# A convolution-and-attention mixer layer laid out anew: order of projections, of convolution taps and of the output rows

## The reference

```python
h = rms_norm_2(x, mix_norm[l]); proj = h @ w_in[l]
a, g, q, k, v, fl = jnp.split(proj, splits, axis=-1)      # 512 each, fl 8
# conv_module(a, g): u = a * sigmoid(g); causal depthwise convolution of 31 taps, 512 channels
#   y = layer_norm(conv(u) + conv_b); y_conv = silu(y)
# forgetting_attention(q, k, v, fl + forget_b): 8 heads of 64,
#   s = q.k/8 + cum[q] - cum[k], cum = cumsum(log_sigmoid(.)); causal softmax; p @ v
y = concat([rms_norm_2(y_conv, onc), rms_norm_2(y_attn, ona)])
x = x + y @ w_out[l]
```

## Time and profile before

| | us |
|---|---|
| median of three runs (lowest, highest) | 1084.83 (1083.31, 1086.01) |
| the profiled execution, its own time | 1083.39 |
| its span, first to last instruction | 1081.6 |
| busy in the span: TensorE, VectorE, ScalarE, GpSimd | 1036.5, 723.3, 617.5, 360.6 |

### The profile page before, as it was taken

How to read it: one execution, slowest core, us unless ns; L and a number is a source line. 1 busy time by engine, 2 the same in 40 slices (tenths; PEclk the granted TensorE clock), 3 DMA queues, 4 the chain that set the end, 5 groups by cost and what they waited for, 6 DMA issues and landing times.

```text
span 1081.6 us, 18110 instructions
## 1 busy us (share of the span) xinstructions
PE 1036.5 (96%) x7606; PEld 972.5 (90%) x7606; DVE 723.3 (67%) x961; ACT 617.5 (57%) x859; POOL 360.6 (33%) x208
## 2 busy tenths in 40 slices
PE   6999999999999899999999999999996899999997
PEld 5889999999987799999999888899986698888886
DVE  5876997773548689877547766643877678665542
ACT  6766666553446566665436555442867966555531
POOL 1062265530100025455102555400387303545400
PEclk9999999999999999999999999999998999999999
DMA  8534664546332346555453755555333155555351
GB/s 317 210 135 159 234 231 158 197 143 233 129 118 78 112 143 237 192 177 198 175 192 118 248 184 193 192 195 175 118 118 116 41 195 188 202 195 195 123 189 39
DMA packets 27297, 183.61 MB, mean 170 GB/s; under 512 B 3152, under 2 KB 3280, under 8 KB 5968
## 3 DMA queue, kind: packets, MB, share of 16 engines
q1 hardware_dynamic: 26784, 181.74, 47.5%
q10 hardware_dynamic: 432, 0.71, 0.2%
HBM read 181.39 MB, written 1.05 MB: 169 GB/s over the span
## 4 chain that ended last, share of the span: by engine, by line
PE 83%; ACT 5%; POOL 4%; DVE 4%; issue 2%; DMA 1%; SPq 0%; DVEq 0%; POOLq 0%; ACTq 0%
PE psum L289 83%; POOL Y L1882 3%; ACT Pb L1004 1%; ACT whi L898 1%; DVE Pb L1460 1%; DMA raw<-in_wst 1%; DVE wlo L1357 1%; ACT Ob L1202 1%; ACT Pb L1211 0%; DVE bias L1363 0%; DVE Pb L1360 0%; ACT L895 0%; POOL LR L1960 0%; PE psum L494 0%; ACT PT L898 0%
## 5 line engine op out<-in xcount | busy, mean ns | idle before, releaser
L289 PE MATMUL psum<-G,whi 128*128 128x256 f32 (+1 forms) x2720 | 614.7, 314 | 12.5 <-DVE wlo L1357 12.5
L1357 DVE TENSOR_TENSOR wlo<-raw,whi 128x2048 fp32r<-128x2048 f32 (+1 forms) x172 | 390.8, 2285 | 217.8 <-ACT whi L898 217.6
L289 PEld LDWEIGHTS psum<-G,whi 128*128 128x128 f32 x2720 | 447.2, 190 | 46.8 <-DVE G L1363 8.5
L289 PE MATMUL psum<-G,wlo 128*128 128x256 f32 x1712 | 482.2, 282 | 0.0
L898 ACT ACTIVATE whi<-raw 128x2048 fp32r<-128x2048 f32 (+1 forms) x172 | 318.5, 1864 | 175.2 <-PE psum L289 168.9
L289 PEld LDWEIGHTS psum<-G,wlo 128*128 128x128 f32 x1712 | 325.0, 190 | 0.1
L1882 POOL TENSOR_TENSOR Alo<-Ab,Ahi 128x512 fp32r<-128x512 f32 x44 | 124.8, 2836 | 139.6 <-ACT Ahi L898 139.6
L1882 POOL TENSOR_TENSOR Ab<-Cb 128x512 f32<-128x512 f32 x44 | 117.5, 2671 | 118.2 <-ACT Cb L939 118.2
L289 PE MATMUL psum<-Ahi,wlo 128*128 128x256 f32 x528 | 149.6, 283 | 0.0
L289 PE MATMUL psum<-Alo,whi 128*128 128x256 f32 x528 | 149.6, 283 | 0.0
L289 PE MATMUL psum<-Ahi,whi 128*128 128x256 f32 x528 | 149.6, 283 | 0.0
(11 more groups left out here) (179 smaller groups left out, 1099.5 us busy)
## 6 DMA issues: line engine op xcount, KB each, us to landing
raw<-in_wst SPq DMA_DIRECT2D x165, 1024.0 KB, 4.9
bias<-in_bias_c SPq DMA_DIRECT2D x1, 2048.0 KB, 8.0
raw<-in_wst SPq DMA_DIRECT2D x3, 512.0 KB, 7.5
X<-in_x SPq DMA_DIRECT2D x4, 256.0 KB, 6.9
raw<-in_wst SPq DMA_DIRECT2D x4, 256.0 KB, 7.1
out<-bias SPq DMA_DIRECT2D x4, 256.0 KB, 2.0
bias<-in_bias_a SPq DMA_DIRECT2D x1, 512.0 KB, 11.1
bias<-in_invcnt SPq DMA_DIRECT2D x1, 512.0 KB, 12.0
```

What stands on the lines that cost most here:

```text
L289: return pe.matmul(o, a, b, start=start, stop=stop, skip_group_check=True)
L1357: return dve.tensor_tensor(o, a, b, op)
```

## The change

Projections now go a1, a2, a0, a3, fl, q0, q1, q2, v0, q3, v1. Tiles 1 and 2 of the convolution take turns on VectorE after a lead of four taps, and VectorE makes the first 20 taps of tile 3 (`early`, in SBUF tile Y), GpSimd the last 11. The forget gate is cut into three pieces placed among the taps; GpSimd starts tile 0 before the factors. In the tail the sums are issued one tile at a time, the attention sums come first, the first rows (two attention tiles) stand between variance sums and square sums, the second behind the square sums, and the attention tiles' scaling and splitting is interleaved with the convolution's norm steps. Two more weight chunks are split ahead of the tail. The core of the diff:

```diff
-    project("w_in", (128, 640))
+    project("w_in", (128, 640), (256, 768), (0, 512), (384, 896))
     plan.append(("heads", "w_in", 2560))
-    project("w_in", (0, 512), (1024, 1536), (256, 768), (384, 896))
-    project("w_in", (1152, 1664), (1280, 1792), (1408, 1920), (2048, 2176), (2304, 2432))
+    project("w_in", (1024, 1536), (1152, 1664), (1280, 1792), (2048, 2176), (1408, 1920), (2304, 2432))
...
+LEAD = 4
+EARLY = 20
-POOL_TAPS = place(*[(0, j) for j in range(31)], *[(3, j) for j in range(30)])
-DVE_TAPS = place(*[(1, j) for j in range(31)], *[(2, j) for j in range(31)], (3, 30))
+POOL_TAPS = place(*[(0, j) for j in range(31)], *[(3, j) for j in range(EARLY, 31)])
+DVE_TAPS = place(*[(1, j) for j in range(LEAD)], *[t for j in range(31 - LEAD) for t in ((2, j), (1, j + LEAD))],
+                 *[(2, j) for j in range(31 - LEAD, 31)])
...
-                value(0)
-                score(3)
-                pe.wait_ge(s_qk, 8 + 4)
-                tokens_first(5, c0 + 10)
-                value(1)
-                turn(2)
-                pe.wait_ge(s_vt, 5)
-                sum_tiles(5, [Y[:, i, :] for i in range(4)], conv_ready, s_xs)
-                value(2)
-                turn(3)
-                sum_tiles(4, [UP[:, i, 0:S] for i in range(4)], lambda n: pe.wait_ge(s_xq, n + 1), s_xs)
-                value(3)
-                pe.wait_ge(s_ptb2, 4)
-                sum_tiles(7, [T[:, i, 0:S] for i in range(4)], lambda n: pe.wait_ge(s_o2, n + 1), s_n)
-                sum_tiles(5, [UP[:, i, 0:S] for i in range(4)], lambda n: pe.wait_ge(s_xq2, n + 1), s_xs)
+                tokens_first(4, c0 + 10)
+                score(3)
+                turn(1)
+                turn(2)
+                value(0)
+                conv_sum(0, 0)
+                value(1)
+                value(2)
+                turn(3)
+                att_sum(0)
+                att_sum(1)
+                value(3)
+                att_sum(2)
+                att_sum(3)
+                conv_sum(1, 1)
+                conv_sum(2, 2)
+                conv_sum(3, 3)
+                var_sum(0)
...
                 rows(0, 2)
+                square_sum(0)
...
                 rows(1, 3)
                 rows(2, 0)
                 rows(3, 1)
...
+                def early(j):
+                    if j == 0:
...
+                        dve.wait_ge(s_tape, j)
+                        STT(Y[:, 3, :], UP[:, 3, j:j + S], col("conv_w", 4 * j + 3), Y[:, 3, :], ALU.mult, ALU.add).then_inc(s_tape, 1)
...
+                early(13)
+                tap(1, 23)
+                early(14)
+                tap(2, 20)
...
+                att_scale(0)
+                center(0)
...
+                att_scale(1)
+                att_low(0)
+                att_scale(2)
+                spread(0)
+                att_low(1)
...
+                        if i == 3 and j == EARLY:
+                            pool.wait_ge(s_tape, EARLY)
...
+                taps(0, 0, 13)
                 pool.wait_ge(s_cum, 1)
                 factors(0)
+                taps(0, 13, 14)
                 factors(1)
+                taps(0, 14, 16)
                 factors(2)
-                taps(0, 0, 26)
+                taps(0, 16, 19)
                 factors(3)
-                taps(0, 26, 31)
-                taps(3, 0, 30)
+                taps(0, 19, 31)
+                taps(3, 20, 31)
...
+                att_factor()
+                att_high(0)
+                conv_square(0)
...
+                att_high(1)
                 conv_factor(0, 4)
+                att_high(2)
+                conv_silu(0)
...
+                att_high(3)
+                high(c0 + 14)
                 table()
                 conv_factor(1, 5)
```

More of the change, by code:

```diff
@@ L508, in values @@
                 last.then_inc(s_pv, 1)
[L510 to L514, removed]
             def l0():
@@ L1278, in mix @@
[L1278 to L1286 removed]
+                products(0, 20, 23)
+                exps(u0 + 1, 1)
+                high(c0 + 11)
+                probs(0)
+                products(0, 23, 25)
+                exps(u0 + 2, 2)
@@ new lines, in mix @@
+                high(c0 + 12)
+                turned(0)
+                products(0, 25, 28)
+                probs(1)
+                products(0, 28, 30)
+                probs(2)
+                products(0, 30, 31)
+                products(3, 20, 21)
+                turned(1)
+                act.wait_ge(s_used, USED[MIX_CHUNK["v1"]])
+                take_v(4, 1, 4)
+                exps(u0 + 3, 0)
+                products(3, 21, 23)
+                turned(2)
+                out(0)
+                high(c0 + 13)
@@ L1308, in mix @@
-                conv_factor(1, 5)
-                high(c0 + 13)
-                for i in range(4):
-                    act.wait_ge(s_on2, 4 + i + 1)
-                    copy(Mhi[:, i, :], Y[:, i, :]).then_inc(s_mh2, 1)
-                high(c0 + 14)
+                products(3, 28, 30)
+                out(3)
+                products(3, 30, 31)
+                att_factor()
+                att_high(0)
+                conv_square(0)
+                conv_square(1)
+                conv_square(2)
@@ L1772, in mix @@
-                taps(1, 21, 22)
+                tap(1, 1)
+                low(c0 + 5)
+                glu(2)
+                tap(1, 2)
+                gates(0)
+                tap(1, 3)
+                tap(2, 0)
+                tap(1, 4)
+                tap(2, 1)
+                low(c0 + 6)
+                glu(0)
+                tap(1, 5)
+                tap(2, 2)
+                tap(1, 6)
+                tap(2, 3)
+                gates(3)
+                tap(1, 7)
+                tap(2, 4)
@@ new lines, in mix @@
+                tap(1, 8)
+                tap(2, 5)
+                tap(1, 9)
+                tap(2, 6)
+                tap(1, 10)
+                tap(2, 7)
+                low(c0 + 7)
+                tap(1, 11)
+                glu(3)
+                forget_sum()
+                tap(2, 8)
+                tap(1, 12)
+                take_q(0)
+                tap(2, 9)
+                early(0)
+                tap(1, 13)
+                tap(2, 10)
+                early(1)
+                tap(1, 14)
@@ L1773, in mix @@
+                early(2)
+                forget_scan()
+                early(3)
+                columns(2)
+                early(4)
+                low(c0 + 8)
+                forget_parts()
+                early(5)
+                tap(2, 11)
+                take_q(1)
+                early(6)
+                tap(1, 15)
+                tap(2, 12)
+                early(7)
+                tap(1, 16)
+                early(8)
+                tap(2, 13)
                 bias_in(0)
-                take_q(1)
@@ L1775, in mix @@
-                glu(3)
-                low(c0 + 8)
+                take_q(2)
                 low(c0 + 9)
-                taps(1, 22, 23)
-                take_q(2)
-                columns(2)
-                taps(1, 23, 24)
+                tap(1, 17)
+                tap(2, 14)
+                tap(1, 18)
                 bias_in(1)
-                taps(1, 24, 25)
-                glu(2)
-                taps(1, 25, 26)
+                tap(2, 15)
+                tap(1, 19)
+                low(c0 + 10)
@@ L1823, in mix @@
-                for i in range(4):
-                    dve.wait_ge(s_mh2, 4 + i + 1)
-                    TT(Mlo[:, i, :], Y[:, i, :], f(Mhi[:, i, :]), ALU.subtract).then_inc(s_m2, 1)
+                tap(1, 20)
+                tap(2, 17)
+                bias_in(2)
+                low(c0 + 11)
+                take_q(3)
+                early(9)
+                tap(1, 21)
+                inverse(1)
+                early(10)
+                low(c0 + 12)
+                inverse(2)
+                tap(2, 18)
```

398 lines of the change are left out of this document (232 added, 166 removed).

## The result

The changed kernel takes 1072.26 us (median of 4 runs, 1071.79 to 1072.71) against 1084.17 (1083.31 to 1086.01) on the same chip: ratio 0.989 [0.987, 0.991], 11.9 us faster. I had said 1076, that is 7.6 us off the profiled execution of before; that profile is now 11.6 shorter. Direction and place were right; the gain is half as large again.

What follows compares the result with a forecast made beforehand. TensorE was held back by GpSimd's convolution adds and VectorE's last tap of tile 3, then by a tail of sums and norms. Middle +0.8 and tail -8.4 gave -7.6 us from 1083.39: 1076 us stated, range 1068 to 1085.

Steps and rivals of the forecast that it cites:

- Ceiling: In the changed stage of 129.4 us, 22.3 us is all that a reordering can win.
- GpSimd: Middle: 18 adds fewer, 15.8 us; start at 785.5, 7 us idle before the factors, tile 3 done at 852.0.
- VectorE: Middle: taps by turns at 0.39 instead of 0.525 us, so 19 extra taps cost nothing.
- Count to the last early tap: Middle, VectorE: its queue counted from 785.5 adds 52.3 us, giving 837.8 before contention.
- The surcharge of 2.6 for contention: Middle, VectorE: 15 early taps meet GpSimd adds at 0.17 us each, putting the last early tap at 840.4.
- The middle: From the stage's start to the end of the conv sums: almost nothing won, 854.0 against 853.2, +0.8 us.
- added 4 for the clock: Middle, TensorE's attention chain: lower clock after gaps moves the last attention sum from 848.6 to 852.6.
- The tail: After the conv sums: 29.1 us instead of 37.5, attention rows running during SiLU work, -8.4 us.
- The 1.3 for the clock at the rows' start: Tail, TensorE: 14 matmuls at the lower clock lose 0.09 us each as the rows begin.
- The first: Whole stage: TensorE bound again, few adds met, clock stays up; -12.9 us, 1070.5, down to 1068; chance 0.20.
- the second rival: Middle: ScalarE's queue as the bound, five tile-3 groups costing 1 us each, 1081 in total; chance 0.12.
- VectorE as the bound: Middle: taps stay at 0.525, early taps wait for whole adds, last early tap 857.2; +7.8 us, 1091; chance 0.09.

Runs made afterwards that it cites:

- experiment 9: The changed kernel run once more, nothing altered: 1072.53 us, ratio 0.988.
- experiment 6: The changed kernel with seven extra matmuls of constants in TensorE's two gaps of the middle: 1069.91 us, ratio 0.986.
- experiment 1: The changed kernel with VectorE's taps of tile 1 all before those of tile 2 instead of by turns: 1074.71 us, ratio 0.991.
- experiment 3: The changed kernel with TensorE's first attention rows behind the square sums instead of before them: 1078.73 us, ratio 0.995.
- experiment 5: The kernel before with only part of the tail's new order, attention rows and their inputs ahead of SiLU and squares: 1082.33 us against 1085.17, ratio 0.998.
- experiment 4: The changed kernel with 24 early taps on VectorE instead of 20 and 7 GpSimd adds of tile 3 instead of 11: 1072.85 us, ratio 0.990.
- 8: The changed kernel with 10 early taps on VectorE instead of 20 and 21 GpSimd adds of tile 3: 1078.27 us, ratio 0.994.
- 10: The changed kernel with both the seven matmuls of constants and 24 early taps, ScalarE's tile 3 products moved up: 1070.68 us, ratio 0.986.
- experiment 11: The changed kernel with constants' matmuls, 24 early taps, products moved up, and a convolution sum ahead of each of the last two attention sums: 1070.44 us, ratio 0.986.

## Why the prediction was right, and where its sizes were off

By its own steps, in its order; times of after less 1.2.

*Ceiling.* 22.3 us were to be had; 12.8 came in the profile, 11.1 in experiment 9's, 13.3 in experiment 6's.

*GpSimd.* 18 adds fewer, and 6.85 idle before the first factor, where I had 7. (The steps that I listed to its start add up to 785.05, not 785.5; it started at 785.6.) Its last add ends at 849.5, not 852.0: the last early tap came 3.2 earlier than I said, and tile 3 took 12.2, not 11.6.

*VectorE.* The pitch of 0.39 came as forecast and experiment 1 shows it (0.525 without the turn). The Trainium skill, "VectorE: DVE Perf Modes", section "The DRAIN you can't avoid", says that the next operation does not start until the pipe is empty and that a semaphore between chained copies costs nothing extra. As I had read it, the turn would win nothing; it won 2.5 us. The same section adds that a next operation that is not held starts earlier, and the gain from the turn agrees with that addition; for taps, a wait for the tap just before costs 0.13. My 8.1 for a turn that fails put 0.525 on all 60 taps; without the turn only 20 of them had it.

*Count to the last early tap.* 837.8 by the count, 837.2 measured, which is partly luck. The six low parts were counted at their mean length of 2.41 and cost 2.2 from start to start (813.38 to 815.58), 1.2 less in all, and that hides what contention did cost. The surcharge of 2.6 for contention was too large: ten early taps meet an add, not 15, and lose 0.9 together from start to next start, 0.5 of it in the one of 0.97; the first, a tensor_scalar, took 0.91 beside an add and lost 0.4 more. So 1.3. The upper bound, a whole add of 0.75 each (which the rule of "SBUF — State Buffer" in the Trainium skill, section "Who interferes with whom", gives), fits the tap of 0.97 and is far off for the other nine, with 0.47 to 0.57. That the early taps write to SBUF and the others to PSUM is not the cause: the nine early ones beside no add take 478 ns, as the others do with 480.

*The middle.* Last attention sum at 849.05; the queues' count gave 848.6, and I had added 4 for the clock. The gaps came (1.52, 2.27, 1.29 for my 1.7, 2.4, 2.3) and so did the lower clock, but only in part of the stretch, and what it cost at the end was 0.5 us in this execution and about 2 in experiment 9, measured from my count (849.31 + 1.52 less the start of 761.40 gives 89.4 after the start, against 87.75 here and 87.3 by the count); from experiment 6, with the clock at 1.00 and 86.6, it is 1.1 and 2.8. Middle: -2.8 (-1.1 in experiment 9) instead of +0.8. **This surcharge is the term that was mis-sized most**: I took the pitch of a stretch behind a gap of 7.86 for one behind gaps of about 2. It is not enough by itself: with the 4 gone, my own GpSimd, done at 852.0, would have held the centring at 852.6. The surcharge on the early taps had to be too large too.

*The tail.* -10.0 instead of -8.4. The 1.3 for the clock at the rows' start did not come: with the pause ahead of the variance sums at 1.02 the window from 851.68 has a clock of 1.00. The rest of the count was right: 27.5 for my 27.7. (The steps that make the convolution tiles ready add up to 5.3, not 5.9, so the 0.1 for them had no ground.) The one place where I saw the risk, square sums behind the first rows, is the one that experiment 3 shows to carry 6.2. What I had not seen is how much of it rests on the middle: in the old middle the same rows ahead of the square sums give 0.5 in the tail of the profile and 2.8 in the medians (experiment 5).

*The rivals.* The first had -12.9 for the stage, my own sum without its surcharges; -12.8 came in this profile and -11.1 in experiment 9's, and the median of 1072.26 lies between its 1070.5 and my 1076. The mechanism is between the two: TensorE is the bound from 852.60 on, not in the 20 us before. ScalarE's queue did not cost the 5 us that the second rival gave it: GpSimd waits 2.8 for it in all, 1.2 of that in tile 3. But the chain of waits runs through it from 821.8 to 842.4, so it is what the middle hangs on there; and at 24 early taps GpSimd waits 3.8 for it if its products are not moved up (experiment 4). VectorE as the bound did not come: its last early tap would have had to end after 849.4, and ended at 837.2.

Not settled: what the gated inputs ahead of the forget gate are worth by themselves. That order was not tried alone, so the middle's parts are told only from experiments 1 (2.5) and 8 (6.0), which overlap with it and with each other. The tail's first part was tried in the old middle without the attention sums in front; how the rest of the 10 us divides between that order and the middle's earlier attention is not told apart. The medians' -11.9 and the stage's -12.8 agree within what the start of the stage moves from one execution to the next.

## What to carry to other kernels

When several surcharges each rest on the nearest bad row, their sum is a rival and not the likeliest case: here the plain count of the queues came within 1 us three times (837.8, with errors that cancelled; 848.6; 27.7), and of the surcharges on the path (4 and 1.3) 0.5 came, which leaves 4.8 of the error of 5.2 (the 2.6 for contention stood on a path that ended just before the other). Work that fills a wait must have its inputs ready by then, and that is decided long before the wait: rows ahead of the square sums took 0.5 us off the tail without the attention's early sums, and carried 6.2 of the 10 with them. When chains end together, read who releases the last wait before shortening one of them; where TensorE's gaps can't be closed with work, matmuls that compute nothing may be worth having for the clock alone, though they do not secure it in each execution.

## What the runs showed of the hardware that I had not expected

- Behind gaps of 2.27 and 1.29 us, in a stretch in which TensorE works only now and then, the granted clock fell (0.66 on average in 838 to 848), and how much of the stretch has the lower level differs between executions of one program (0.54 in experiment 9). With matmuls of constants that cut these gaps to 0.55 and 0.53 it was 1.00 in the profiles of experiments 6 and 10, and the kernel 2.3 to 2.6 us faster; in the profile of experiment 11, with the same constants, it fell to 0.79 in 848 to 852. The Trainium skill, "TensorE: Matmul & The Clock Gate", section "What's actually happening", says that the throttled state is the default and activity releases it; these rows agree.
- A wait of 3.10 us ahead of the rows in experiment 5 costs another 2.4 behind it, in rows at the lower level.
- Ten taps that read two SBUF tiles while GpSimd adds took 0.08 us more on the mean than nine that met no add (559 and 478 ns); one of them took 0.97, the others at most 0.57.
- Two chains of taps by turns, into the two halves of PSUM bank 2, do not disturb each other: 0.39 from one tap to the next, where each waiting for the one before has 0.525.
